# Softmax denominators of a hybrid encoder step: turnings and sums against products with a column of ones

## The reference

```
s = einsum('bqhd,bkhd->bhqk', q, k) * HEAD_DIM ** -0.5 + cq - ck
p = softmax(where(mask, s, -inf), axis=-1)
out = einsum('bhqk,bkhd->bqhd', p, v)
```

## Time and profile before

| | us |
|---|---|
| median of three runs | 1409.5 (1409.11 to 1409.52) |
| the profiled execution | 1408.32 |
| its span | 1406.4 |
| TensorE busy | 1369.0 (97%) |
| VectorE busy | 922.0 (66%) |
| ScalarE busy | 636.6 (45%) |
| GpSimd busy | 575.6 (41%) |

### The profile page before, as it was taken

How to read it: one execution, slowest core, us unless ns; L and a number is a source line. 1 busy time by engine, 2 the same in 40 slices (tenths; PEclk the granted TensorE clock), 3 DMA queues, 4 the chain that set the end, 5 groups by cost and what they waited for, 6 DMA issues and landing times.

```text
span 1406.4 us, 25060 instructions
## 1 busy us (share of the span) xinstructions
PE 1369.0 (97%) x8382; PEld 1086.1 (77%) x8382; DVE 922.0 (66%) x2025; ACT 636.6 (45%) x1364; POOL 575.6 (41%) x606
## 2 busy tenths in 40 slices
PE   8999999999999999999999999999999999999998
PEld 7999767788877777777777777777777777778886
DVE  3789755593376778666433676776776776497775
ACT  6766423332353354445333455555555655422121
POOL 2122442200033234221100556877977867644452
PEclk9999999999999999999999999999999999999999
DMA  7885699987349769787998767448458355556552
GB/s 234 295 281 199 201 268 252 275 273 228 113 139 272 248 223 266 243 266 237 313 321 264 170 189 158 107 98 181 103 109 181 83 114 196 160 169 199 191 177 89
DMA packets 211023, 284.21 MB, mean 202 GB/s; under 512 B 49809, under 2 KB 146481, under 8 KB 207409
## 3 DMA queue, kind: packets, MB, share of 16 engines
q1 hardware_dynamic: 209856, 282.61, 68.7%
q10 hardware_dynamic: 1040, 0.00, 0.0%
HBM read 191.12 MB, written 90.19 MB: 200 GB/s over the span
## 4 chain that ended last, share of the span: by engine, by line
PE 60%; DVE 3%; POOL 2%; ACT 2%; issue 2%; DMA 2%; SPq 1%; DVEq 0%; ACTq 0%; POOLq 0%
PE in_g L927 14%; PE attn_pv L2531 10%; PE attn_s L2601 6%; PE attn_s L2500 6%; PE attn_s L2505 5%; PE attn_pv L2601 5%; PE attn_s L2485 5%; PE attn_s L2513 2%; PE in_b L1102 1%; POOL in_hv L1810 1%; PE in_b L1054 1%; PE attn_s L2554 1%; PE attn_s L2502 1%; PE in_b L1157 1%; PE in_b L1122 1%
## 5 line engine op out<-in xcount | busy, mean ns | idle before, releaser
L927 PE MATMUL in_g<-in_wh,in_xh 128*128 128x512 f32 (+2 forms) x904 | 331.4, 380 | 6.2 <-ACT in_xh L1219 2.4
L927 PE MATMUL in_g<-in_wl,in_xh 128*128 128x512 f32 (+2 forms) x904 | 321.9, 369 | 0.0
L2807 POOL TENSOR_TENSOR attn_probs<-attn_probs,attn_probs_turned 128x512 f32<-128x512 f32 (+3 forms) x200 | 214.3, 1072 | 64.9 <-ACT attn_probs_turned L2633 40.9
L927 PE MATMUL in_g<-in_wh,in_xl 128*128 128x512 f32 (+2 forms) x904 | 236.4, 380 | 1.4 <-DVE in_xl L1532 1.3
L2847 DVE TENSOR_REDUCE attn_tops<-attn_s 128x1 f32<-128x512 f32 (+3 forms) x288 | 159.1, 596 | 108.6 <-PE attn_s L2485 108.6
L2633 ACT ACTIVATE attn_probs_turned<-attn_s 128x512 f32<-128x512 f32 (+1 forms) x352 | 161.2, 545 | 125.7 <-PE attn_s L2505 124.8
L927 PEld LDWEIGHTS in_g<-in_wh,in_xh 128*128 128x128 f32 x904 | 165.5, 189 | 40.8 <-issue 7.4
L927 PEld LDWEIGHTS in_g<-in_wl,in_xh 128*128 128x128 f32 x904 | 165.6, 189 | 27.9
L927 PEld LDWEIGHTS in_g<-in_wh,in_xl 128*128 128x128 f32 x904 | 159.1, 190 | 34.9 <-issue 5.3
L1808 POOL TENSOR_SCALAR in_hs<-in_hs 128x8 f32<-128x8 f32 (+1 forms) x53 | 19.5, 368 | 401.8 <-DVE in_hs L1559 401.8
L2531 PE MATMUL attn_pv<-attn_probs_turned,attn_v 128*64 128x256 f32 (+1 forms) x1216 | 142.1, 363 | 0.0
(11 more groups left out here) (377 smaller groups left out, 2685.8 us busy)
## 6 DMA issues: line engine op xcount, KB each, us to landing
in_xu<-scratch_xt SPq DMA_DIRECT2D x87, 512.0 KB, 5.4
in_xl<-scratch_xt SPq DMA_DIRECT2D x34, 512.0 KB, 4.6
in_raw<-in_w_in SPq DMA_DIRECT2D x40, 256.0 KB, 5.2
scratch_xt<-in_xu SPq DMA_DIRECT2D x19, 512.0 KB, 4.4
scratch_xt<-in_xl SPq DMA_DIRECT2D x17, 512.0 KB, 5.0
scratch_k<-in_x_turned SPq DMA_DIRECT2D x17, 512.0 KB, 7.2
scratch_q<-in_x_turned SPq DMA_DIRECT2D x17, 512.0 KB, 5.4
in_x_turned<-in_x_prompt SPq DMA_DIRECT2D x16, 512.0 KB, 4.8
```

The costliest lines, as they stand in the source:

```text
L927: last = X.matmul(g_ps[b][:, 0:m], x, ws[:, c, w0:w0 + m], start=(c == 0 and h == 0 and ws is wh), stop=(c == KC - 1 and h == 1))
L2807: E.tensor_tensor(acc[:, part:, :], acc[:, part:, :], mine, ALU.add).then_inc(added[engine], 1)
```

## The change

The step den on TensorE no longer turns the four tiles of `acc`. For each it computes a product whose stationary operand is the tile and whose streamed operand is `K.one`, a column of 128 ones. The result is one column of 128 sums, one for each query, written to column i of the bank. VectorE's sum and the buffer `den` go; the reciprocal reads four columns of the bank. The semaphore `s_denr` goes too: the bank is given back, and the output projection's third product of the first pair starts, on `s_rden`, which the reciprocal raises.

```diff
@@ -2106,7 +2106,6 @@
             negmax = over.sb("negmax", [P, 2, P], F32R)
         probs = a.sb("probs", [P, 2, 4, 4, P])
         top_parts = a.sb("tops", [P, 2, EACH, 5])
-        den = a.sb("den", [P, 2, EACH])
 
         rfox, rmem = a.sb("rfox", [P, PROMPT_TILES, FOX_HEADS]), a.sb("rmem", [P, PROMPT_TILES, MEM_HEADS])
 
@@ -2149,7 +2148,7 @@
         s_fill, s_load = [a.sem(f"fill{h}") for h in range(2)], [a.sem(f"load{h}") for h in range(2)]
         s_mx, s_top, s_neg, s_row, s_rowc = (a.sem(k) for k in ("top_scores", "top", "negmax", "row", "row_copied"))
         s_score, s_exp, s_pv, s_copy = (a.sem(k) for k in ("scores", "exp", "values", "out_copied"))
-        s_addp, s_addv, s_den, s_denr, s_rden = (a.sem(k) for k in ("added_p", "added_v", "den", "den_read", "rden"))
+        s_addp, s_addv, s_den, s_rden = (a.sem(k) for k in ("added_p", "added_v", "den", "rden"))
         s_store = [a.sem(f"stored{h}") for h in range(2)]
         s_vload = [a.sem(f"values_loaded{h}") for h in range(2)]
         LOADS, VLOADS, STORES, FILLS = 7, 8, 4, (3, 6)
@@ -2214,7 +2213,7 @@
 
         def emptied(what, i):
 
-            return {"scores": (s_exp, i + 1), "top": (s_top, i + 1), "row": (s_rowc, i + 1), "den": (s_denr, i + 1)}[what]
+            return {"scores": (s_exp, i + 1), "top": (s_top, i + 1), "row": (s_rowc, i + 1), "den": (s_rden, i + 1)}[what]
 
         def folds_upto(o):
 
@@ -2510,7 +2509,7 @@
                     pe.wait_ge(added[engine], n)
                     acc = acc_v[:, sums.at[s], :, :] if s in sums.at else acc_p[:, s % 4, :, :]
                     for i in range(EACH):
-                        last = X.transpose(bank[:, i, :], acc[:, i, :], K.ident[:, :])
+                        last = X.matmul(bank[:, 0, i:i + 1], acc[:, i, :], K.one[:, 0:1], start=True, stop=True)
                     last.then_inc(s_den, 1)
                 if what == "values":
                     u, k, part = scores[s]
@@ -2578,7 +2577,7 @@
                         else:
                             pe.wait_ge(s_sum, sums_upto(q - 1, 0))
                     if q == 1 and j == 2:
-                        pe.wait_ge(s_denr, ALL)
+                        pe.wait_ge(s_rden, ALL)
                     if q > 1 and j == 2:
                         pe.wait_ge(s_y, y_upto(q - 1, 2))
                     if q and j == 3:
@@ -2866,13 +2865,9 @@
                 if what == "den":
                     u = units[s]
                     dve.wait_ge(s_den, s + 1)
-                    if s >= 2:
-                        dve.wait_ge(s_rden, s - 1)
-                    V.tensor_reduce(den[:, s % 2, :], ring_ps[ring.at[what, s]][:, :, :], AX.X, ALU.add).then_inc(s_denr, 1)
-                    dve.wait_ge(s_denr, s + 1)
                     at = u.first + (u.head % 2 * (MQ // P) if u.kind == "mem" else 0)
                     by = rmem[:, at:at + EACH, u.head // 2] if u.kind == "mem" else rfox[:, at:at + EACH, u.head]
-                    V.reciprocal(by, den[:, s % 2, :]).then_inc(s_rden, 1)
+                    V.reciprocal(by, ring_ps[ring.at[what, s]][:, 0, 0:EACH]).then_inc(s_rden, 1)
                 if what == "fold":
 
                     o, u = s, s % 2
```

## The result

| | before | after |
|---|---|---|
| median, side by side (4 runs each) | 1409.3 us (1406.65 to 1409.52) | 1433.97 us (1431.59 to 1436.19) |
| ratio | | 1.0179 (95%: 1.0159 to 1.0200) |
| profiled run, span | 1408.32, 1406.4 | 1433.54, 1431.5 |
| mean granted clock of TensorE | 0.997 | 0.991 |

The change costs 24.7 us where 16.9 were forecast; the time lies at the top edge of the range, and outside the forecast's own range of 1421 to 1430.

What follows compares the result with a forecast made beforehand. TensorE was taken to pace the attention stage: 43.0 us of loads less 21.1 of turnings and 4.0 at the ends gives +17.9, less VectorE's 1.0 is +16.9, so 1426 us from a median of 1409.5; range 1416 to 1434.

Steps and rivals of the forecast that it cites:

- TensorE sets the time, VectorE is beside it: In the attention stage TensorE paces all others, busy 390.62 of 391 us; VectorE idles 108.6 us before the maxima.
- VectorE's busy time falls by some 32 us: Sign to look for in the profile after the change, with VectorE's idle time growing.
- 192 turnings at 0.110 us, 21.1 us: In the steps den of 48 attention units, the removed turnings take 21.1 us of TensorE's path.
- VectorE's sums worth 1.0 us (0 to 2.2): Dropping 48 sums, 32.7 us of VectorE beside TensorE's work, gives back only part of TensorE's 2.2 us of waits.
- 384 loads, two for a plain float32 product: The 192 new products on TensorE need two weight loads each, where a turning has one.
- 0.112 us a load, given by the load and not by the stream: For one-column products on TensorE the weight load is the limit; 384 loads take 43.0 us.
- rival 1: Each load of the new products is dearer, 0.13 us: +23.8 us, 1433 us; chance 0.12.
- 2 (0.06): Rival: loads overlap better, with a period of 0.06 us: 1409.5 us, no change; chance 0.05.
- 3 (0.028): Rival: TensorE's weight path takes only 0.028 us a load, so the kernel gets faster, 1394 us; chance 0.05.
- rival 4: Each one-column product has a single load, not two: -4.6 us, 1405 us; chance 0.03.
- 4.0 us given back at the ends, net +17.9 on TensorE: At the ends of 40 stretches the last column streams for nearly nothing; 43.0 - 21.1 - 4.0 = +17.9 us.
- Nothing else moves: No DMA touched, no wait added on TensorE; the last step's extra 0.45 us goes into a 1.9 us wait.

Runs made afterwards that it cites:

- split: The changed kernel with at most one step den in a cycle, so places of eight products become four and four: 1422.89 us, ratio 1.0104; repeated 1423.55 us, 1.0121.

## Why the prediction was wrong

1. **TensorE sets the time, VectorE is beside it**: right. The stage is as full after as before (419.62 and 419.38 of 420 us), and 30 us less on VectorE alone bought nothing. Of the sign "VectorE's busy time falls by some 32 us" 27 came, as its additions grew longer.
2. **192 turnings at 0.110 us, 21.1 us**: right; doubling them cost 0.44 and 0.87 us a place.
3. **VectorE's sums worth 1.0 us (0 to 2.2)**: mis-sized; no gain shows (ratio 1.0014, 0.9999 to 1.0030). The ten waits of the earlier trace rows stand unchanged without the sums, so they come from the maxima that the rows name.
4. **384 loads, two for a plain float32 product**: right, counted in the trace.
5. **0.112 us a load, given by the load and not by the stream**: right. Loads start 0.112 us apart, and 128 columns in place of one add 0.10 us to a whole place of four or eight. Rivals 1 (0.13), 2 (0.06) and 3 (0.028) are out, and rival 4 (one load) only comes true with one-pass operands. The median of 1434 looks like rival 1's 1433; the trace shows that it isn't: the places have the forecast's length.
6. **4.0 us given back at the ends, net +17.9 on TensorE**: right; 17.8 measured.
7. **"Nothing else moves"**: this step failed. The sum took the granted clock of 1.00 in the earlier trace rows as given, though the change takes away almost all that streamed in 40 places. After it the clock falls to 0.50 five times for 3.4 us each, and TensorE, which paces the stage, pays 1.6 us for each, 8 in all. With the clock's term and without VectorE's, the sum is 17.8 + 8 = 26, where the spans differ by 25.1 and the medians by 24.7. The small part of this step was off as well: the last step's 0.45 us were to vanish in the wait at L2554, which only shrinks from 1.9 to 1.7 us.

What the trace of before could have said: its one fall stood behind idle time of TensorE, and nothing in it shows one while PE is busy. So the size couldn't be had from it, but a rival could: 40 places in which next to nothing streams any more, eight of them 1.7 us long, and for each fall a few microseconds at half speed. For the Trainium skill, "TensorE: Matmul & The Clock Gate", section "HAM oscillation — how this bites in real kernels", it is idle gaps of TensorE that bring the clock down. The fall at 251 us agrees, and the one at 792 us after the change stands behind idle time too. The four behind places of eight don't agree, since TensorE's busy share stood at 1.00 before and through each. The fifth had 0.33 us of idle time before it, but the same wait stands in the trace of before (0.34 us at 890 us) and no fall follows it there. So a busy share of 1.00 on the page is no sign that the clock is held.

Still open: why the clock falls behind some places of eight and not others, why a place of four has one (at 897 us in both profiles), and why 32 columns had one there. That the falls go with little streaming is shown by the runs with one, 32 and 128 columns, by the doubled turnings and by those that keep the places short, each with one profile and the mean clock of its runs; what in the chip brings the clock down isn't shown.

## What to carry to other kernels

On TensorE a short product costs its weight loads, not its columns: count loads (two for plain float32, one for fp32r), at 0.112 us each for 128x128. Before a long stream is replaced by a very short one in a stage that TensorE paces, add a term for the clock (here 1.6 us a fall), look at the granted clock in stretches of 1 us afterwards, and keep short products apart from each other or give them one pass. The clock over a long stretch hides a fall: 1.00 over 420 us leaves room for one. Work taken off an engine that idles beside the bound buys nothing; read from the waits which of its instructions is really late.

## What was not expected of the hardware

- A granted clock of 0.50 for 3.4 us behind sixteen matmuls of one column (1.68 us of them), with PE busy 1.00: four and five times in two profiles, and once more in each behind eight of them that follow a wait of 0.3 us. With 128 columns, turnings included, never in the attention; with 32 once; in the kernels that never have more than eight short matmuls in a row, split or in one pass, never in the attention.
- A matmul of one column with new weights takes 0.112 us of the stream and is recorded with up to 0.27 us.
- Two loads of 128x128 for one plain float32 column are as dear as two turnings (0.224 against 0.22 us), which is why this way to sum over partitions loses to the turnings in plain float32 and wins in one pass.
